# Second mixer's attention: when VectorE takes a finished output from PSUM, relative to its other work in a step

## The reference, cut to what matters

```python
o_cmp, p_cmp = compressed_branch(q, kcmp, vcmp, slopes)   # 63 compressed keys
idx = selection_indices(p_cmp, s)                         # 8 of 16 blocks of 64, per position and group
o_sel = selected_branch(q, ks, vs, idx, slopes)           # keys of the selected blocks
o_win = window_branch(q, kw, vw, slopes)                  # the last 512 positions
g = sigmoid(gate)
o = g[..., 0:1] * o_cmp + g[..., 1:2] * o_sel + g[..., 2:3] * o_win
```

## Time and profile before

| | |
|---|---|
| median of 3 runs | 3408.33 us (3407.6 to 3408.38) |
| the profiled execution's own time | 3407.07 us |
| its span | 3405.3 us |
| the attention stage | from about 1064 to 1415 us of the span |
| busy over the span | PE 94%, DVE 46%, ACT 21%, POOL 2% |
| mean granted clock | 0.955 |

### The profile page before, as it was taken

One profiled execution on the slowest core, in us unless ns is written; L12 is line 12 of the kernel. 1 busy time (PEld: TensorE's weight loads), 2 busy tenths in 40 slices (PEclk: granted clock), 3 DMA queues, 4 the chain that ended last, 5 costly groups with the idle time before them and its releaser, 6 DMA issues.

```text
span 3405.3 us, 38439 instructions
## 1 busy us (share of the span) xinstructions
PE 3199.2 (94%) x16063; PEld 2515.3 (74%) x16063; DVE 1552.9 (46%) x2294; ACT 713.6 (21%) x1194; POOL 75.0 (2%) x147
## 2 busy tenths in 40 slices
PE   4899999996998999899999999989989899999999
PEld 3787865553655988677888888868857788888887
DVE  6434125624114456534443343378983534434434
ACT  3232235512112555411000000021142100000001
POOL 1000000100004000000000000000000000000000
PEclk8999999997898999799999999989989999999999
DMA  7001110012110000111111111101100211111111
GB/s 287 19 20 45 35 25 16 16 62 74 38 38 10 1 1 1 69 50 62 44 50 46 46 49 49 43 19 50 38 14 25 74 50 50 49 49 37 49 49 50
DMA packets 138666, 153.29 MB, mean 45 GB/s; under 512 B 27015, under 2 KB 126251, under 8 KB 137003
## 3 DMA queue, kind: packets, MB, share of 16 engines
q1 hardware_dynamic: 136704, 134.40, 12.4%
q10 hardware_dynamic: 1835, 17.11, 1.2%
HBM read 138.91 MB, written 12.58 MB: 44 GB/s over the span
## 4 chain that ended last, share of the span: by engine, by line
PE 55%; DVE 2%; ACT 1%; issue 0%; DVEq 0%; ACTq 0%
PE ps L1225 42%; PE ps L1202 10%; PE ps L1298 1%; DVE sc L2349 0%; PE ps L1351 0%; PE ps L1335 0%; PE ps L730 0%; DVE h_low L2353 0%; PE ps L760 0%; DVE sc L1851 0%; ACT big L1791 0%; ACT h_high L1809 0%; ACT sc L1812 0%; DVE h_low L2485 0%; DVE big L2482 0%
## 5 line engine op out<-in xcount | busy, mean ns | idle before, releaser
L1225 PE MATMUL ps<-h_high,w_high 128*128 128x512 f32 x1408 | 550.4, 391 | 15.0 <-DVE h_low L2353 15.0
L1225 PE MATMUL ps<-h_high,w_low 128*128 128x512 f32 x1408 | 549.9, 391 | 0.0
L1225 PE MATMUL ps<-h_low,w_high 128*128 128x512 f32 x1408 | 549.7, 390 | 0.0
L1202 PE MATMUL ps<-h_high,ring_parts 128*128 128x512 f32 x1024 | 322.4, 396 | 22.5 <-DVE h_low L2353 9.0
L1225 PEld LDWEIGHTS ps<-h_high,w_high 128*128 128x128 f32 x1408 | 265.7, 189 | 70.6 <-issue 15.4
L1225 PEld LDWEIGHTS ps<-h_low,w_high 128*128 128x128 f32 x1408 | 265.7, 189 | 55.4
L1225 PEld LDWEIGHTS ps<-h_high,w_low 128*128 128x128 f32 x1408 | 265.8, 189 | 55.3
L1754 ACT ACTIVATE sc<-ps 128x1024 f32<-128x1024 f32 x44 | 45.3, 1030 | 1237.0 <-PE ps L1225 1237.0
L2329 DVE TENSOR_TENSOR xt<-ps,xt 128x1024 f32<-128x1024 f32 x176 | 211.5, 1221 | 145.5 <-PE ps L1225 145.5
L1225 PE MATMUL ps<-act_high,w_high 128*128 128x512 f32 x704 | 273.9, 389 | 0.0
L1225 PE MATMUL ps<-act_high,w_low 128*128 128x512 f32 x704 | 273.9, 389 | 0.0
(11 more groups left out here) (362 smaller groups left out, 4504.1 us busy)
## 6 DMA issues: line engine op xcount, KB each, us to landing
ring<-in_ffn_w_gate_dram SPq DMA_DIRECT2D x22, 1024.0 KB, 5.1
ring<-in_ffn_w_up_dram SPq DMA_DIRECT2D x22, 1024.0 KB, 5.2
ring<-in_ffn_w_down_dram SPq DMA_DIRECT2D x22, 1024.0 KB, 4.7
ring<-in_conv_w_pw_dram SPq DMA_DIRECT2D x24, 512.0 KB, 3.8
x_kept<-xt ACTq DMA_DIRECT2D x2, 4096.0 KB, 12.0
xt<-x_kept ACTq DMA_DIRECT2D x2, 4096.0 KB, 12.1
ring<-in_w_mod_dram SPq DMA_DIRECT2D x4, 1536.0 KB, 15.2
ring<-in_w_in_dram SPq DMA_DIRECT2D x10, 512.0 KB, 3.7
```

The source lines that it names most:

```text
L1202: last = mm(bank(banks + half), (hi, lo)[wp_][:, k, :], h_part[rp_][:, k, 512 * half:512 * half + 512], start=k == 0 and p_ == 0, stop=k = ...
L1225: return mm(o, w, rows, start=start and part_ == 0, stop=stop and part_ == 2)
```

## The change

In VectorE's loop of that stage, `n_outs` of unit s-4 moves from the end of a step to its beginning. Nothing else changes: the same instructions, waits and semaphores in another order on one engine.

```diff
             for step in range(N_NSA + 5):
+                if 0 <= step - 4 < N_NSA and nsa_units[step - 4].last:
+                    n_outs(nsa_units[step - 4])
                 if step < N_NSA:
                     un = nsa_units[step]
                     n_biases(un)
                     if un.kind == "win" and un.h in (1, 3):
                         selection(un.i, un.h // 2)
                 if 0 <= step - 1 < N_NSA and nsa_units[step - 1].kind == "cmp":
                     c_normed(nsa_units[step - 1])
-                if 0 <= step - 4 < N_NSA and nsa_units[step - 4].last:
-                    n_outs(nsa_units[step - 4])
             stage(v, "mixer_attended")
```

## The result

| | before | after |
|---|---|---|
| median | 3408.33 us | 3427.04 us (3423.67 to 3429.85, 5 runs) |
| ratio | | 1.0056, 95% interval 1.0041 to 1.0071 |
| profiled execution and its span | 3407.07 and 3405.3 us | 3427.04 and 3425.3 us |
| mean granted clock | 0.955 | 0.952 |

The change makes the kernel 18.7 us slower. The sign was forecast, the size was not: the sum said 8.5 us, and the range ended at 3424.

A forecast was written before the change was run, and what follows sets the result against it. TensorE was taken to bound the attention stage. Terms of 0.8, 7.3 and 0.4 us, with 0 for the clock, summed to 8.5 us, giving a median of 3416.8 us; the range was 3406 to 3424.

The forecast's parts named there:

- What bounds the kernel: Attention stage: TensorE is the bound, busy 312.66 of 351 us; it waits 17.7 us at 7 block starts for an output.
- the 7 waits of 3 to 4 us: Sign of being right: at block starts, TensorE waits for copies or exponentials replace its waits for the output.
- The delayed bias: Sign of being right: in steps 9, 13 and 17 of narrow blocks, biases start 0.6 to 0.9 us after their scores end.
- Part 1: Output at the start of a block, 7 times: 0.8 us slower in all, from the three wide starts; narrow ones 0.
- Part 2: Outputs of units 5, 9 and 13 in every block, 24 in all: 7.3 us slower.
- The first block: Outputs of units 0 and 1 in the first block: 0.4 us slower for unit 0, nothing for unit 1.
- The clock: Slow stretches at 1.2 GHz behind TensorE's stops at block starts: 0 in the sum, between -5 and +6 us.
- slower by the clock as well: Rival, chance 0.10: at four of six full-speed starts more path work runs at the lower clock, +7 us, 3424 us.
- Absorbed: Rival, chance 0.35: each output's 0.4 to 0.5 us is won back within some steps; 3413.1 us, within 0.2%.
- Faster: Rival, chance 0.08: the 17.7 us of TensorE waits at block starts vanish and nothing replaces them; 3390.6 us.

The follow-up runs named there:

- experiment with the swapped copies: Kernel before with only unit 17's output moved, plus ScalarE's copies of unit 2 ahead of unit 4's exponentials in later blocks: 3399.78 us, ratio 0.9979.
- fillers: Extra TensorE transposes at block starts: 24 (wide) or 10 (narrow) in the changed kernel, 3417.90 us, or with only output 17 moved, 3406.99; 20 in the kernel before, 3402.52.
- output 17 alone: Kernel before with only the output of unit 17 moved ahead of the bias of step 3: 3419.94 us, ratio 1.0026.
- cutting the long piece of work that everything waited for: Kernel before with its two selections cut into three parts each, in steps 4, 5, 6 and 7, 8, 10: 3380.37 us, ratio 0.9923.

## Why the prediction was right in sign and wrong in size

**What bounds the kernel**, right: the 17.7 us of the earlier trace rows were not to be had, since the copy on ScalarE stands behind them. The transposes of step 5 came 0.17 us later at i = 6, 0.2 were forecast. The experiment with the swapped copies shows the cause, which the prediction only argued from the 0.49 us of the earlier trace rows. Of the signs named, the 7 waits of 3 to 4 us came as two shorter ones at each start (1.72 and 2.65 us at i = 6, 2.14 and 0.93 at i = 3), for copies as said. The delayed bias came as said: 0.71 us behind its scores at i = 3, with VectorE's idle time ended by L1153.

**Part 1**, right in its mechanism, rather short in size: 0.8 us forecast. With fillers on both sides the move of output 17 costs 1.4 us by the traces, 3.6 by the medians (3406.99 and 3402.52 us, each against its own runs before) and more by the ratios, so the order is not shown to be free. In the changed kernel's trace the seven starts are 3.0 us longer, 1.3 of it at i = 5 and 0.2 to 0.5 in each of the narrow ones, where I had put 0.

**Part 2**, right in its mechanism, short in one term. Forecast per output and measured: i = 5, 0.25 and 0.25; i = 4, 0.44 and 0.49; i = 3, 0.53 and 0.60. The term that was mis-sized is the 0.4 for i = 2, 1 and 0, where I let part of the delay go into waits for copies that were there already. Measured 0.72, 0.74 and 0.49: those waits did not take it up. 7.3 us forecast; 9.5 by the distances, 10.4 by the traces of the pair of kernels with fillers (11.9 by their medians).

**The first block**, 0.4 forecast; by the trace it is 0.8 us longer.

**The clock** is the step that failed. I put 0 in the sum "between -5 and +6 us", on the ground that the slow stretch would as often come off the path as onto it. It did not: TensorE's busy time at the lower clock rose from 31.9 to 45.1 us, its busy time in the stage by 6.0 us, and the fillers price the clock's share at 5.4 us by the traces and 3.2 by the medians, the ratios leaving it open. The bounds that I had given hold that, toward their upper end: what failed is the zero. In the forecast each lost microsecond was a wait of TensorE; in the trace a third of them are the same products running slower. The rows do show that the slow stretches became longer in sum, 34 to 51 us. With output 17 alone they sum to 54.6 us, so that move, which puts the values and scores ahead of the stop, is enough to bring it about. Why it does is not shown. One can think that before, the slow stretch fell on values and scores with slack behind them: at the starts of i = 6, 5 and 4 waits of 0.49, 0.30 and 1.17 us followed them. But at i = 3, 2 and 1 none followed, and in the changed kernel the slow stretches of i = 4, 3 and 2 again begin with values and scores, with waits of 1.46, 0.93 and 0.94 us behind. So this can be a part of it at most.

The rival "slower by the clock as well" had the mechanism with +7 us and a chance of 0.10, and its 3424 is the nearest of the forecast times. It would still have been short: in the traces the 17.9 us are 0.8 for the first block, 1.4 for output 17, 10.4 for the other outputs and 5.4 for the clock, where the forecast had 0.4, 0.8, 7.3 and 0. These four add up by construction, and each is good to a few microseconds only. All the misses went the same way; by the traces the clock's is the largest and the outputs' 3.1 us come next, by the medians the outputs' is the larger (11.9 for 7.3).

**The other rivals.** Absorbed: no; narrow blocks give nothing back. Faster: no, and the point from which it would decide was right, for with the copies ahead of the exponentials the kernel does get faster.

## What to carry to other kernels

Before a wait is taken away, ask what the engine will want next and behind what that is queued; here one reordering alone loses and together with a second one wins, and cutting the long piece of work that everything waited for wins more (3380.37 us against 3399.78). An item that becomes ready only when the bias's own input starts to be made does not belong ahead of the bias, even if it is early in the program: put it where the engine is idle anyway. And of a stop of TensorE count the work that follows it as well: behind the stops of both kernels it ran at half the clock for 3.4 to 13.7 us. How a reordering changes the length of that stretch could not be forecast from the trace of before, so a term for it wants a price and not a zero.

## What the runs showed of the hardware that was not expected

After a stop the lower clock can last long although TensorE is nearly always busy: 13.60 us at 0.50 with 11.52 busy in the changed kernel, at other starts 10.3 or 6.8, and 3.4 in the kernel before, with much the same work behind them. Nothing in these traces tells which it will be. The Trainium skill, "TensorE: Matmul & The Clock Gate", section "HAM oscillation", describes such kernels, where each stop makes the next work start cold. The traces agree: in both kernels the clock is at 0.50 to 0.55 behind all six starts between the first and the last block.

Useless work in the stop can be worth its place: 20 transposes at each of 7 starts made the kernel before 5.2 us faster (ratio 0.9974, 0.9962 to 0.9985). But it must not be longer than the stop: with 24 in the changed kernel the starts took 77.6 us, with 24 or 10 they took 72.5.
